# Turning query and key heads by a VectorE block transpose and SBUF transfers, with the first two output tiles interleaved

## The reference

```python
for layer in range(DEPTH):                     # DEPTH = 2
    xn = rms_norm(x, attn_norm[layer])
    x = x + (mixer_ab(xn, ...) if layer % 2 == 0 else mixer_cd(xn, ...))
    x = x + swiglu(rms_norm(x, ffn_norm[layer]), w_gate[layer], w_up[layer], w_down[layer])
```

## Time and profile before

| | |
|---|---|
| median of 3 runs | 2149.07 us |
| time of the profiled execution | 2148.37 us |
| its span | 2146.6 us |
| TensorE busy | 2129.5 us (99%) |
| VectorE busy | 1380.5 us (64%) |
| ScalarE busy | 1001.7 us (47%) |
| GpSimd busy | 65.8 us (3%) |
| TensorE clock granted | 1.000 |

### The profile page before, as it was taken

The page is one execution under the profiler, slowest core; times in us unless marked ns, Lnnn a source line. Parts: engine busy times, 40 slices in busy tenths (PEclk is TensorE's granted clock), DMA queues, the critical chain, the costliest instruction groups (busy, mean ns, idle before and its releaser), DMA issues.

```text
span 2146.6 us, 28247 instructions
## 1 busy us (share of the span) xinstructions
PE 2129.5 (99%) x9540; PEld 1760.2 (82%) x9540; DVE 1380.5 (64%) x1807; ACT 1001.7 (47%) x1270; POOL 65.8 (3%) x55
## 2 busy tenths in 40 slices
PE   8999999999999999999999999999999999999999
PEld 7888888888888888888888778888888888888887
DVE  5755587676666766666666666786676666765443
ACT  6555555444444444444455556454444444444443
POOL 0000010000000000000011010000000000000000
PEclk9999999999999999999999999999999999999999
DMA  8545556666666665555665453466666666656654
GB/s 275 167 147 172 172 176 196 195 183 191 204 195 182 190 204 185 186 190 193 210 192 176 147 158 118 157 199 194 194 183 191 203 195 183 189 189 203 215 201 141
DMA packets 207805, 399.32 MB, mean 186 GB/s; under 512 B 13312, under 2 KB 13568, under 8 KB 207744
## 3 DMA queue, kind: packets, MB, share of 16 engines
q1 hardware_dynamic: 205296, 394.30, 59.4%
q10 hardware_dynamic: 2448, 4.21, 0.6%
HBM read 396.37 MB, written 2.10 MB: 186 GB/s over the span
## 4 chain that ended last, share of the span: by engine, by line
PE 96%; DVE 2%; ACT 1%; issue 0%; POOL 0%; DMA 0%; SPq 0%; ACTq 0%; DVEq 0%
PE psum L411 31%; PE psum L414 31%; PE psum L412 31%; PE psum L501 2%; PE psum L431 1%; PE psum L479 1%; ACT w_hi L578 1%; DVE w_lo L836 1%; DVE turn_sb L882 0%; POOL head_rstd L1156 0%; PE psum L499 0%; DMA x_res<-in_x 0%; ACT xt_hi L621 0%; DVE xt_lo L894 0%; DVE stage L976 0%
## 5 line engine op out<-in xcount | busy, mean ns | idle before, releaser
L836 DVE TENSOR_TENSOR w_lo<-w_raw,w_hi 128x1024 fp32r<-128x1024 f32 x760 | 908.5, 1202 | 625.8 <-ACT w_hi L578 620.4
L578 ACT ACTIVATE w_hi<-w_raw 128x1024 fp32r<-128x1024 f32 x760 | 786.3, 1041 | 937.0 <-PE psum L414 925.1
L411 PE MATMUL psum<-w_hi,xt_hi 128*128 128x512 f32 x2016 | 795.6, 395 | 3.8 <-DVE xt_lo L894 3.6
L414 PE MATMUL psum<-w_hi,xt_lo 128*128 128x512 f32 x2016 | 785.5, 390 | 0.0
L412 PE MATMUL psum<-w_lo,xt_hi 128*128 128x512 f32 x2016 | 784.8, 389 | 0.0
L411 PEld LDWEIGHTS psum<-w_hi,xt_hi 128*128 128x128 f32 x2016 | 378.8, 188 | 83.4 <-DVE xt_lo L894 4.8
L414 PEld LDWEIGHTS psum<-w_hi,xt_lo 128*128 128x128 f32 x2016 | 378.6, 188 | 79.7
L412 PEld LDWEIGHTS psum<-w_lo,xt_hi 128*128 128x128 f32 x2016 | 378.9, 188 | 77.8
L411 PE MATMUL psum<-w_hi,ht_hi 128*128 128x512 f32 x960 | 376.1, 392 | 0.0
L414 PE MATMUL psum<-w_hi,ht_lo 128*128 128x512 f32 x960 | 373.7, 389 | 0.0
L412 PE MATMUL psum<-w_lo,ht_hi 128*128 128x512 f32 x960 | 373.6, 389 | 0.0
(11 more groups left out here) (98 smaller groups left out, 606.7 us busy)
## 6 DMA issues: line engine op xcount, KB each, us to landing
w_raw<-in_w_gate SPq DMA_DIRECT2D x176, 512.0 KB, 3.7
w_raw<-in_w_up SPq DMA_DIRECT2D x176, 512.0 KB, 3.8
w_raw<-in_w_down SPq DMA_DIRECT2D x160, 512.0 KB, 4.2
w_raw<-in_cd_w_in SPq DMA_DIRECT2D x80, 512.0 KB, 3.8
w_raw<-in_ab_w_in SPq DMA_DIRECT2D x72, 512.0 KB, 3.7
w_raw<-in_ab_w_out SPq DMA_DIRECT2D x32, 512.0 KB, 3.6
w_raw<-in_cd_w_out SPq DMA_DIRECT2D x32, 512.0 KB, 3.6
w_raw<-in_w_down SPq DMA_DIRECT2D x32, 256.0 KB, 2.6
```

The costliest lines, as they stand in the source:

```text
L411: nc.tensor.matmul(acc, hi[:, chunk, ts], w_hi[:, slot, c, :], start=first and c == 0, stop=False)
L414: mm = nc.tensor.matmul(acc, lo[:, chunk, ts], w_hi[:, slot, c, :], start=False, stop=end)
L578: nc.scalar.activation(w_hi[:, slot, 0:n, :], w_raw[:, slot, 0:n, :], ACT.Copy).then_inc(hi_ready, 1)
L836: nc.vector.tensor_tensor(w_lo[:, slot, 0:n, :], w_raw[:, slot, 0:n, :], w_hi[:, slot, 0:n, :].bitcast(F32), ALU.subtract).then_inc(lo_rea ...
```

## The change

The q and k heads no longer go through TensorE. VectorE turns the scaled and rotated tile by 32x32 blocks in one instruction (`blocks`, in tick tk, right behind the rotation), and SP moves the blocks to their partitions with sixteen transfers of 32 partitions (32 KB each, 16 KB for kv_b), eight ahead of the load of unit tk+8 and eight ahead of that of unit tk+9 (`move_qk`). Keys land where the scores read them, with a block layout (`keys` reads runs of 32 elements). Queries land in `land_sb` and ScalarE copies them into order in one instruction of 128x1024, in attention tick tk+6 (tk+5 for q_a and k_a; the latter is scaled in place by the product of both gains). The squares are summed, the power taken and the heads scaled in two halves, one for each token half.

The first two output tiles are interleaved: four units of tile 0, four of tile 1 (in `ACC[1]`), and again. So the heads' ticks may reach eight units further (`PAIR_UNITS`), and all head ticks move: the first head of b from 22 to 25, of d from 37 to 41, of c from 61 to 65. The residual of tile 0 then falls due after 12 units and that of tile 1 after 16. The probabilities have one PSUM bank for their transposes in place of two, the late heads of layer 1 two banks for scores, and the `xt_lo` of an output tile's last residual is made at unit 6 and not at unit 7 of the phase behind it (and that of layer 0's last down tile).

```diff
+OUT_UNITS = [(n, k) for half in range(2) for n in range(2) for k in range(4 * half, 4 * half + 4)]
+OUT_UNITS += [(n, k) for n in range(2, XT) for k in range(KU)]
@@ SP
+            def move_qk(layer, v):
+                m = mixers[layer]
+                for q, p in enumerate(m.qk_tiles):
+                    _, kind, h0 = m.tiles[p]
+                    run = TOK * 32 * (2 if kind == "kv_b" else 4)
+                    at = m.qk_tick(p, 2) + RING + LEAD + 1
+                    if v in (at, at + 1):
+                        if v == at:
+                            sp.wait_ge(qk_blocks, m.qk0 + q + 1)
...
+                        for b in range(2 * (v - at), 2 * (v - at) + 2):
+                            for a in range(4):
+                                sp.dma_start(dst[32 * b:32 * b + 32, a], turn_sb[32 * a:32 * a + 32, b, 0:run]
+                                             ).then_inc(qk_landed, 16)
...
+                        move_qk(layer, KU * p + k)
                         load(u, k % RING, w_in[layer], UC * k, UC, slice(col * N, col * N + N), first=u < RING)
@@ TensorE
-                for q, p in enumerate(m.qk_tiles):
-                    if t == m.turn_tick(p):
...
-                                transposes(lambda c, tok: src[:, tok, (2 * half + c) * P:(2 * half + c + 1) * P], f)
...
-                        wait_read(pe, m.fill["qk", p, 0], m.fill["qk", p, 1])
+                        pe.wait_ge(qk_ready, m.finish_rank[p] + 1)
...
-                                mm = nc.tensor.matmul(dst, qt[:, qh, tok * P:tok * P + P], kt[:, kh, :],
+                                mm = nc.tensor.matmul(dst, query(kind, qh, tok), keys(kind, kh),
@@ ScalarE
+                    if t == m.qk_tick(p, 8 if kind[-1] != "a" else 7) and p in m.finish_rank:
+                        act.wait_ge(qk_landed, 256 * (m.qk0 + q + 1))
+                        if kind != "k_a":
+                            dst = query_tile(kind, h0).rearrange("p t c (a i) -> p (t c) a i", a=4)
+                            src = land_sb[:].rearrange("p a t c i -> p (t c) a i")
+                            nc.scalar.activation(dst, src, ACT.Copy).then_inc(qk_ready, 1)
+                            continue
@@ VectorE
+            def blocks(layer, q, kind):
...
+                    src = stage[2 if kind in ("q_a", "k_a") else 0]
+                    dst = turn_sb[:].rearrange("p b (g i) -> p g b i", g=TOK * 4)
+                    ins = nc.vector.transpose(dst, src[:].rearrange("p t (c b j) -> p (t c) b j", c=4, b=4))
+                ins.then_inc(qk_blocks, 1)
...
+                    for n in range(XT - 1):
+                        late = i - OUT_END[n] - LEAD
+                        if 0 <= late < 4:
+                            turn(layer, "out", n, late)
+                        if late == 5:
+                            residual_lo(layer, "out", n)
```

More of the change, by code:

```diff
@@ L88, in __init__ @@
         self.fill = {}
[L89 to L94, removed]
+        for t in range(self.ticks):
             for n, (_, _, _, at, _) in enumerate(items):
@@ L305, in wait_read, with o_bank, keys_tensor, query_tile @@
                 eng.wait_ge(t_read[f % 2], f // 2 + 1)
[L308 to L313, removed]
+        def o_bank():
+            return psum[:, OBANK, 0:SEQ]
         def heads_of(s, n):
             return s[:, :, 0:n * DH].rearrange("p t (h d) -> p t h d", d=DH)
[L319 to L324, removed]
+        def keys_tensor(kind):
+            return {"kv_b": kt_b, "k_a": kt_a, "k_c": kt_c, "k_d": kt_d}[kind]
+        def query_tile(kind, h0):
+            return {"q_b": qt_b, "q_a": qt_a, "q_c": qt_c, "q_d": qt_d}[kind][:, h0 // 4]
+        def query(kind, h, tok):
+            return {"a": qt_a, "b": qt_b, "c": qt_c, "d": qt_d}[kind][:, h // 4, tok, h % 4, :]
+        def keys(kind, h):
+            kt = {"a": kt_a, "b": kt_b, "c": kt_c, "d": kt_d}[kind]
+            return kt[:, h // 4, :, :, h % 4, :].rearrange("p a t i -> p t a i")
         def pt_of(layer, n):
@@ L385, in _ @@
                                 sp.dma_start(dst, src).then_inc(loaded, 16)
[L386 to L389, removed]
+                for i, (n, k) in enumerate(OUT_UNITS):
+                    move_qk(layer, KU * len(m.tiles) + i)
+                    load(ph["out", layer]["u"] + i, i % RING, w_out[layer], m.chunks[UC * k], UC,
+                         slice(n * N, n * N + N))
                 with sp.Fori(0, HT) as i:
@@ L749, in _ @@
                 m, pi, po, pu, pd = mixers[layer], *(ph[s, layer] for s in ("in", "out", "up", "down"))
-                def out_tile(n, first):
-                    for k in range(KU):
-                        if k == LEAD and first:
-                            evacuate(layer, len(m.tiles) - 1)
-                        split(n * KU + (po["u"] + k), k % RING)
-                        if first:
-                            attention(layer, KU * len(m.tiles) + k - LEAD)
-                        elif k == LEAD + 2:
-                            residual_ssq(layer, "out", n - 1)
-                        elif k == LEAD + 3:
-                            residual_hi(layer, "out", n - 1)
                 for p in range(len(m.tiles)):
@@ L781, in _ @@
                             act.dma_start(cd_gain_sb[:], cd_gain).then_inc(cd_const_loaded, 16)
-                out_tile(0, True)
-                for t in range(m.ticks - LEAD, m.ticks + 2):
-                    attention(layer, t)
-                with act.Fori(0, XT - 1) as j:
-                    out_tile(j + 1, False)
+                for i in range(len(OUT_UNITS)):
+                    if i == LEAD:
+                        evacuate(layer, len(m.tiles) - 1)
+                    split(po["u"] + i, i % RING)
+                    if i < PAIR_UNITS:
+                        attention(layer, KU * len(m.tiles) + i - LEAD)
+                    for n in range(XT - 1):
+                        if i == OUT_END[n] + 7:
+                            residual_hi(layer, "out", n)
+                        if i == OUT_END[n] + 6:
+                            residual_ssq(layer, "out", n)
                 def up_tile(i, first):
```

274 lines of the change are left out of this document (144 added, 130 removed).

## The result

The changed kernel takes 2191.7 us, the median of four runs (2191.0 to 2192.5), beside 2149.0 for the kernel before in runs of its own: a ratio of 1.020, 95% interval 1.0187 to 1.0213. It is slower than the kernel before, and far beyond the forecast of 2152.9 and its range of 2138 to 2163. The profiled execution took 2191.76 us, 43.4 more than the one of before.

What follows compares the result with a forecast made beforehand. TensorE's matmul pitch was taken as the bound. Gains of -20.3, +5.0 for interleaved output tiles and +19.1 for lateness gave +3.8 on 2148.37, 2152.2, plus 0.7 for the median: 2152.9 us; 8-in-10 range 2138 to 2163.

Steps and rivals of the forecast that it cites:

- the issue time of the sixteen transfers: SP's queue: 0.48 us per issue delays weight loads behind the moves; the stops for late loads and heads sum to +19.1 us.
- output phase: Interleaved output tiles: VectorE falls behind, 2.4 us of stops around units 20 to 22 plus 0.1, both layers: +5.0 us.
- the heads' stops: Layer 1, d and c heads: late row maxima, a wait for banks and late transposes, 0.8, 2.0 and 0.3 us, within the +19.1.
- Transposes off TensorE: Head transposes: 112 leave TensorE, 14 groups at 0.90 us plus 0.45 for kv_b: -13.0 us.
- the first q_b stop: TensorE's stop behind the first q_b rotation, 0.93 us idle, goes with the transposes: -1.1 us.
- `xt_lo` earlier: Move from a residual's last tile to the next phase: three TensorE stops of 1.2+0.16 us vanish: -4.1 us.
- Head ticks: Attention heads: TensorE's stops for probabilities, 1.33 and 0.51 us, go as the ticks move, with 0.16 each: -2.1 us.
- rival 3: VectorE's block transpose takes 1.74 us, or the finishing copy is slow: +5 us, 2158 us; chance 0.09.
- Loads behind the moves: SP's queue: the weight load behind eight moves lands 3.8 us after its issue, if the moves are out of its way.
- rival 2: Weight loads land later, waiting in the same queue for 256 small packets and receipts: 15 us more, 2167 us; chance 0.11.
- rival 4: Reading keys in runs of 32 elements doubles the time of the score matmuls: 2180 us; chance 0.03.
- Rival 1: Lateness swallowed: at about 0.4 us an issue or less, loads come in time: 2137 to 2143 us; chance 0.29.

Runs made afterwards that it cites:

- the kernel that has the price I assumed: The changed kernel with its sixteen moves a tile read from x in device memory, not from turn_sb, so the tile's values are left out: 2163.5 us, ratio 1.0071.

## Why the prediction was wrong

**The step that failed** is the issue time of the sixteen transfers: "I take 0.48 for each", "whatever the size". The mechanism, the queue and the waits were right; the size of this term was not. 0.48 was read from loads out of device memory, the only ones on SP's queue that the trace of before had back to back, and for these it is right: 0.474 and 0.464 in the runs that read from there. From SBUF to SBUF it is 0.633. The range had bounds for the issue time below (0.41, nothing) and none above. I had priced the operation by the nearest row without asking in what that row differed. The 0.47 and 2.2 us that the prediction holds against each other as issue and landing are not of one transfer either: the first is `gain_a` of 1 KB on SP's queue, the second `gain_x` of 16 KB on ScalarE's.

**Its slope was right.** "0.07 us of it is worth 10 us": the two changed kernels that differ in the source alone are 28.3 us apart for 0.17, so 0.07 is worth 11.7.

**The rest of the sum** can now be read from the kernel that has the price I assumed: 2163.5 against 2152.9, 10.6 too much. Of these, 3.2 are slow matmuls behind stops, which no term of mine had; 2.4 are the output phase; and 1.6 are the heads' stops, 4.7 with the 0.16 of each where I had 3.1. The remaining 3.4, by subtraction, lie in the stops for late loads themselves and in small ones. The steady q_d tile returned after 25.7 and 25.1 us, close to the 24.7.

**What stands between the two**, 28.3 us, is more than later loads: the slow matmuls grew from 3.2 to about 12. Of the ten stops of 2.7 to 4.2 us in the changed kernel, eight had slow matmuls behind them, of those up to 2.0 none.

**Point by point.**
- Transposes off TensorE, -13.0: held. The groups cost 14.1 in the trace of before, with the first q_b stop's 1.1 in it.
- `xt_lo` earlier, -4.1: held; alone it gives 4.9 (interval 2.8 to 6.9).
- Head ticks, -2.1: did not come as a net gain; with one transfer a tile 2.9 us of such waits stand in the list (2.3 for `probs`, 0.6 for `sinkexp`), more than the 1.8 of before. The sums above count the old stops as gone and these as new.
- Block transpose 1.25 us and finishing copy 1.05: held, rival 3 is out.
- Loads behind the moves landing in 3.8: 4.2 in the median of the thirty, 3.8 to 5.6, a small part of rival 2.
- Output phase, +5.0: 3.7 a layer and not 2.5. `w_lo` of unit 20 was late by 1.4 (forecast 1.8), but the last wait, 1.65 at unit 24 for tile 2's residual, was not in my sum, which ended at unit 22.
- Keys in runs: the 48 score matmuls of kind d take 380 ns each, as before, and start 0.218 apart, as before; rival 4 is out.
- Rival 1, all swallowed below 0.43 an issue: at 0.464 the stops are still there; lower was not tried with sixteen; with one transfer a single stop of 1.5 us for `evacuate` is left.

The Trainium skill, "DMA: Bandwidth & Descriptors", section "Issuing engines are not separate DMA queues", has the time to initiate a DMA as usually small beside the DMA itself; for these transfers of 32 KB it is a third, 0.59 against 1.8 us. By its "Rules for kernel authors", joining small transfers, the runs agree: 2191.7 with sixteen, 2151.7 with five, 2143.5 with one.

## What to carry to other kernels

Price a transfer's issue, not only its landing, by a row with the same source and destination; where none exists, leave the upper end of the range open, and multiply by all that is queued ahead of a load with a deadline. Sixteen small transfers in the queue that also feeds the weights cost more than the 0.9 us a tile of TensorE's time that they saved. A stop can cost more than its length: behind most of those of 3 and 4 us here TensorE soon ran at half its clock. And of a bundle of edits each should be tried alone, since the one gain here that needed nothing else (`xt_lo` a unit earlier, 4.9 us) was buried under 48.

## What the hardware showed that I had not expected

- Back to back on SP's queue, a transfer from SBUF to SBUF follows the one before by 0.633 us (0.644 with 128 partitions); the same transfer out of device memory by 0.464 (one of 128 KB by 0.474). The load behind such a transfer shares its fate: its issue takes 0.58 behind one from SBUF to SBUF, 0.42 behind one out of device memory, and 0.37 alone. A single transfer of 512 KB takes 0.47 from SBUF to SBUF and 0.34 from SBUF to device memory.
- GpSimd issued the same transfers 0.49 apart, paused 4 to 6 us within four of the fifteen tiles, and they landed after 3.6 us instead of 1.8.
- After a stop of 4.0 us, TensorE's granted clock was 0.50 for ten matmuls; 5 to 10 such matmuls stood behind most of the long stops, 1.0 to 2.3 us each time; behind one there were two or three. The length of a stop doesn't settle it: in the changed kernel two of 2.9 and 3.1 us (at 1124.6 and 1295.6) and the one of 2.0 at 1278.4 had none, while in the kernel with one transfer a tile six slow matmuls with weights follow one of 2.0:

```profile
1236.54 0.85 PE L478 MATMUL psum<-ident_sb,probs 128*128 128x128 f32 x4 [1.86 <-DVE probs L1069]
...
1238.05 0.63 PE L461 MATMUL psum<-w_hi,xt_lo 128*128 128x512 f32 x1
1238.47 0.63 PE L458 MATMUL psum<-w_hi,xt_hi 128*128 128x512 f32 x1
```
